# Each 512 KB weight chunk of a two-layer diffusion step loaded by two transfers of 256 KB

## What is computed

```python
for l in range(2):
    mc, ml = adaln(c_ctx, ada_w[l], ada_b[l]), adaln(c, ada_w[l], ada_b[l])   # shift, scale, gate, twice
    h = modulate(x, norm_mix[l], shift, scale)             # RMS norm, then scale and shift
    y = retention_mixer(h) if l == 0 else windowed_attention(h)
    x = x + gate * y
    h = modulate(x, norm_ffn[l], shift2, scale2)
    x = x + gate2 * conv_ffn(h)                            # 1024 -> 2 x 2816, conv of 3, silu(g) * u, -> 1024
y = rmsnorm(x, norm_final)
```

## Time and profile before

| | |
|---|---|
| median of 3 runs | 2172.25 us (2169.92 to 2173.08) |
| the profiled execution's own time | 2175.08 us |
| its span in the trace | 2173.3 us |
| TensorE matmul busy | 2057.9 us, 95% of the span |
| queue of the weight stream (q1) | 171.99 MB in 47232 packets, 23.1% of 16 engines' span |
| mean granted TensorE clock | 0.97 |

### The profile page before, as it was taken

One profiled execution on the slowest core, in us unless ns is written; L12 is line 12 of the kernel. 1 busy time (PEld: TensorE's weight loads), 2 busy tenths in 40 slices (PEclk: granted clock), 3 DMA queues, 4 the chain that ended last, 5 costly groups with the idle time before them and its releaser, 6 DMA issues.

```text
span 2173.3 us, 32383 instructions
## 1 busy us (share of the span) xinstructions
PE 2057.9 (95%) x12472; PEld 1809.2 (83%) x12472; DVE 925.8 (43%) x1299; ACT 654.1 (30%) x1280; POOL 758.0 (35%) x477
## 2 busy tenths in 40 slices
PE   5899999999999998999999999997779999999998
PEld 3776888598688757999999999984449999999998
DVE  1511410340242044762464364654441774575473
ACT  2522212223222224331232233334432432232232
POOL 1433233233323323333233334336654333333332
PEclk9899999999999998999999999898989999999999
DMA  6432232223123201432432342220002122222211
GB/s 238 171 136 78 97 107 78 77 91 105 68 98 116 68 29 40 154 137 78 145 115 102 113 144 69 75 74 1 1 1 68 52 79 78 73 77 78 68 68 49
DMA packets 52265, 190.02 MB, mean 87 GB/s; under 512 B 5825, under 2 KB 6977, under 8 KB 51521
## 3 DMA queue, kind: packets, MB, share of 16 engines
q1 hardware_dynamic: 47232, 171.99, 23.1%
q10 hardware_dynamic: 4928, 16.53, 2.0%
HBM read 181.41 MB, written 7.08 MB: 87 GB/s over the span
## 4 chain that ended last, share of the span: by engine, by line
PE 88%; DVE 3%; issue 3%; ACT 2%; DMA 1%; POOLq 1%; POOL 1%; DVEq 1%; ACTq 0%; SPq 0%
PE ps L350 35%; PE ps L389 21%; PE ps L365 15%; PE ps L405 2%; PE ps L332 2%; PE ps L541 2%; PE ps L550 1%; PE ps L423 1%; DVE stat L1394 1%; PE ps L536 1%; PE ps L337 1%; PE ps L413 1%; PE ps L710 1%; ACT pr L1007 1%; POOLq L1077 1%
## 5 line engine op out<-in xcount | busy, mean ns | idle before, releaser
L1051 POOL TENSOR_TENSOR w_l<-raw,w_h 128x1024 fp32r<-128x1024 f32 x232 | 563.4, 2430 | 1173.9 <-ACT w_h L746 1173.6
L350 PE MATMUL ps<-h_h,w_h 128*128 128x320 f32 x1696 | 528.3, 311 | 3.1 <-issue 1.6
L350 PE MATMUL ps<-h_h,w_l 128*128 128x320 f32 x1696 | 524.7, 309 | 0.0
L350 PE MATMUL ps<-h_l,w_h 128*128 128x320 f32 x1696 | 524.7, 309 | 0.0
L746 ACT CAST w_h<-raw 128x1024 fp32r<-128x1024 f32 x232 | 245.5, 1058 | 580.9 <-PE ps L389 315.6
L350 PEld LDWEIGHTS ps<-h_h,w_h 128*128 128x128 f32 x1696 | 319.0, 188 | 16.4 <-issue 14.7
L350 PEld LDWEIGHTS ps<-h_l,w_h 128*128 128x128 f32 x1696 | 319.1, 188 | 0.2 <-issue 0.2
L350 PEld LDWEIGHTS ps<-h_h,w_l 128*128 128x128 f32 x1696 | 319.1, 188 | 0.0
L1344 DVE SCALAR_TENSOR_TENSOR cc<-ca,vec,cc 128x641 f32<-128x641 f32 x88 | 231.1, 2627 | 15.2 <-issue 15.2
L1203 DVE SCALAR_TENSOR_TENSOR xT<-ps,mods,xT 128x128 f32<-128x128 f32 (+2 forms) x264 | 107.8, 436 | 302.7 <-PE ps L389 302.7
L389 PE MATMUL ps<-m_l,w_h 128*128 128x320 f32 x704 | 216.8, 308 | 0.0
(11 more groups left out here) (183 smaller groups left out, 2720.1 us busy)
## 6 DMA issues: line engine op xcount, KB each, us to landing
raw<-stream_dram SPq DMA_DIRECT2D x328, 512.0 KB, 3.6
S<-state_dram ACTq DMA_DIRECT2D x4, 1024.0 KB, 7.7
new_state_dram<-st_out ACTq DMA_DIRECT2D x8, 512.0 KB, 3.1
xT<-x_dram ACTq DMA_DIRECT2D x1, 2560.0 KB, 12.1
y_dram<-aq ACTq DMA_DIRECT2D x8, 320.0 KB, 2.4
dm<-diff_dram ACTq DMA_DIRECT2D x1, 512.0 KB, 4.7
rope_t<-rope_t_dram ACTq DMA_DIRECT2D x1, 512.0 KB, 8.7
rope_a<-rope_a_dram ACTq DMA_DIRECT2D x1, 512.0 KB, 3.7
```

The lines of the kernel that those rows point to most:

```text
L350: mm = nc.tensor.matmul(ps[:, banks + half, 0:HALF], w, x[:, k, lo_hi(half)], start=(k == 0 and n == 0), stop=(k == KT - 1 and n == 2))
L1051: nc.gpsimd.tensor_tensor(w_l[:, r, :], raw[:, s, :], w_h[:, r, :].bitcast(F32), ALU.subtract).then_inc(raw_used[s], 1)
```

## The change

Every chunk is loaded by two transfers, partitions 0 to 63 and partitions 64 to 127, issued one behind the other on the same queue after the same wait. Both add 16 to the same semaphore, so its two waiters ask for 32 for each chunk. Nothing else is changed.

```diff
@@ -300,7 +300,8 @@
                 s = c % RAW
                 if turns is not None:
                     sp.wait_ge(raw_used[s], turns)
-                sp.dma_start(raw[:, s, :], dr["stream"][c + RAW * i]).then_inc(raw_landed[s], 16)
+                for rows in (slice(0, P // 2), slice(P // 2, P)):
+                    sp.dma_start(raw[rows, s, :], dr["stream"][c + RAW * i, rows]).then_inc(raw_landed[s], 16)
@@ -398,7 +399,7 @@
                 for kc in range(4):
                     s, n = b.chunk(b.ada[k0 + kc], i)
-                    pe.wait_ge(raw_landed[s], 16 * n)
+                    pe.wait_ge(raw_landed[s], 32 * n)
@@ -740,7 +741,7 @@
                 s, landed = b.chunk(b.at[j], i)
                 r, n = b.split(j, i)
-                act.wait_ge(raw_landed[s], 16 * landed)
+                act.wait_ge(raw_landed[s], 32 * landed)
```

## The result

The changed kernel takes 2194.03 us (median of 4 runs, 2186.75 to 2197.21) against 2172.36 us of the kernel before: a ratio of 1.0095, 95% interval 1.0075 to 1.0116. It is slower by 21.7 us by the medians, 16.3 to 25.2 by the interval. The forecast was 2187 (2173.5 to 2200): the direction and the mechanism are right; the forecast loss, 15 us, is two thirds of what came.

The account below looks back on a forecast made before the run. TensorE, busy 95% of the span, was taken as the bound, so loads matter only where it waits for them. FFN 7.2 + 0.2, retention 0.7 and start 7.3 sum to 15.4 us: 2172.25 + 15.4 = 2187.6, say 2187 us (2173.5 to 2200).

Parts of the forecast that it names:

- d: Added delay until a whole chunk has landed, taken as 0.9 us between bounds of 0.1 and 1.43, at half rate per half.
- The distance in a burst: Time between landings of chunks issued in a row: 1.43 us before, forecast 1.43 + 0.9 = 2.3 us.
- The start: Loads up to the first projection: chunk 11 4.4 us late, chunk 19 2.4, cst 0.5; together 7.3 us.
- for cst I add 0.5 us (0 to 2): At the start, cst shares the DMA engines with the four first chunks; its delay was put at 0.5 us.
- where TensorE wants it at 33.3: At the start, chunk 11 would land at 37.7 us but is wanted at 33.3: 4.4 us lost.
- The shift for chunk 19: Chunks 16 to 19, issued from 48.6 us: the fourth lands at 60.0 in place of 57.6, delaying the first projection 2.4 us.
- The retention: Four ada blocks whose last chunk has 0.84, 0.76, 0.39 and 0.87 us to spare: 0.7 us lost in all.
- the FFN: Layer 0: eight already waiting ada blocks pay 8 x 0.9 = 7.2 us; two with 0.88 and 0.74 us in hand, 0.2.
- a microsecond there is covered: ACT's waits for main chunks, which TensorE needs four main chunks later; a tile takes 7.1 us, so small delays cost nothing.
- Full rate for each half: Rival: 64 partitions load as fast as 128, delay 0.15 us, 2 us lost, 2174 us, not slower; chance 0.24.
- Fully one after the other: Rival: halves wholly serial, delay 1.43 us, bursts 2.86 us apart, 31 us lost, 2203 us; chance 0.18 for delay above 1.2.
- the sign that was named for "wrong": Around a chunk loaded alone, GB/s still reaching 400 and more would mean the half rate is wrong and time near 2174.

## Why the prediction was right, and where it fell short

*d, right.* The forecast took 0.9 us between bounds of 0.1 and 1.43; it is 0.95 (4.60 against 3.64). Its reason, half the rate for half the partitions, read off stores that were not a clean comparison, is borne out in kind: with even and odd partitions, and with the middle 64, the slow packets are gone. But the makeup was not as told. I put the difference down to the rate alone; the rate gives 0.6 us, and 0.3 us is a part that I had left out: a transfer of 64 partitions holds SP for 0.47 us and starts its packets 0.3 us later. That the chosen value came out right is partly luck: the rate was taken too dear, and the longer issue at nothing.

*The distance in a burst, right.* The four chunks of the second ada block land at 23.2, 25.6, 27.8 and 30.1 us, 2.3 us apart, as forecast. Its last was forecast at 28.5.

*The start, 9.1 us for 7.3: two terms mis-sized.* The step "for cst I add 0.5 us (0 to 2)" measured 1.5 us: TensorE's first block starts at 16.48 for 14.95, and chunk 4 is issued that much later. The other is "where TensorE wants it at 33.3". That is the first matmul that uses chunk 11. Its weight load, which waits for the chunk, starts at 32.40 before, 0.9 us sooner. Chunk 11 now lands at 38.96, 1.3 us later than forecast. So the third block ends 6.6 us later (40.93 for 34.33): 4.4 us of the forecast, 1.3 and 0.9. The chain of the changed kernel, 14 to 42 us, goes this way:

```profile
16.48 1.95 PE ps L406 x6
...
23.28 6.78 DMA raw<-stream_dram
30.10 1.84 PE ps L406 x4
...
32.75 6.21 DMA raw<-stream_dram
39.01 1.95 PE ps L406 x4
```

The forecast also left out chunks 0 to 3, which before were there when TensorE wanted them. The fourth now lands at 20.56, and its weight load starts 2.4 us later than at the pace of before (PE, 16 to 24 us):

```profile
16.48 3.95 PE L406 MATMUL ps<-raw,csil 128*32 128x512 f32 x12 [16.48 <-DMA cst<-cst_dram]
20.60 1.44 PE L406 MATMUL ps<-raw,csil 128*32 128x512 f32 x4 [0.17 <-DMA raw<-stream_dram]
```

This stall isn't on the chain: chunk 4 is released by the block's first matmuls, and the loads behind it are issued without a wait.

The shift for chunk 19 was right: issued 6.55 us later and landed 8.9 later, 2.4 us more. The last conversion ends at 67.5 in place of 58.6, and the first projection starts at 69.7 for 61.0, where the forecast had about 7 us. TensorE's clock, which I let move along, did not. The slow stretch (granted clock 0.50, 1.2 of 2.4 GHz) ends 5.4 us later, at 72.6 for 67.2, so less of the projection runs in it: from there to the fifth ada block it is 15.6 us for 17.3. Then from 87 to 97 us the granted clock averages 0.66, 6.8 us of the ten at 1.2 GHz and the others at 2.4, where before such a stretch lasts 3.4 us: from the fifth block to the sixth it is 30.8 us for 28.7. The two nearly cancel.

*The retention, 3.1 us for 0.7, and the FFN, 8.3 + 1.0 for 7.4: the same step failed, "with 0.84, 0.76, 0.39 and 0.87 us to spare" and "two have 0.88 and 0.74 us in hand".* I took the time in hand from the landing to the first matmul of the chunk. It is the weight load, though, that waits for the semaphore, and it is issued one chunk ahead of its matmul. The last weight loads of the same block, before and then after:

```profile
1043.62 0.14 PEld L405 LDWEIGHTS ps<-raw,csil 128*32 128x32 f32 x4 [0.30 <-issue]
1044.05 0.13 PEld L405 LDWEIGHTS ps<-raw,csil 128*32 128x32 f32 x4 [0.29 <-issue]
```

```profile
1059.65 0.12 PEld L406 LDWEIGHTS ps<-raw,csil 128*32 128x32 f32 x2 [0.31 <-issue]
1060.16 0.14 PEld L406 LDWEIGHTS ps<-raw,csil 128*32 128x32 f32 x4 [0.39 <-DMA raw<-stream_dram]
```

Before, the last chunk's weight load starts at 1044.05 and the chunk has landed at 1043.60: 0.44 us in hand, not 0.88. With 0.44 us less everywhere, the retention's four come to 0.5 + 0.6 + 0.9 + 0.5 = 2.5 us (measured inside the blocks: 0.3, 0.8, 0.8 and 1.0; three of these chunks landed 4.7 to 4.9 us after their issue, not 4.5) and the FFN's two to 0.5 + 0.6 (measured 0.5 and 0.6). The eight blocks that waited already paid 0.8 to 1.1 us each, as forecast, but for one: the block at 904.38 us pays 1.9. Its last chunk is issued 1.4 us before the block, where it was 2.3, and that is a second step that failed: that "a microsecond there is covered" for main chunks. The block before it, the 14th, follows the norm, and there ACT has caught up with the stream and waits for the next main chunk. That chunk landed 4.76 us after the 14th block's start and now lands 5.70 us after it, and ACT converts it 0.94 us later:

```profile
872.15 1.05 ACT L746 CAST w_h<-raw 128x1024 fp32r<-128x1024 f32 x1 [2.18 <-DMA raw<-stream_dram]
```

```profile
885.24 1.05 ACT L747 CAST w_h<-raw 128x1024 fp32r<-128x1024 f32 x1 [3.12 <-DMA raw<-stream_dram]
```

For the next 13 us the instructions of ACT, VectorE and GpSimd that stand behind it are 0.93 us later too, by both timelines. At the end is the conversion of GpSimd that frees the slot of the late chunk: it ends 23.29 us after the 14th block's start, for 22.37. TensorE's tiles have not moved: the next ada block starts 24.86 us after the 14th in both traces. So this block pays d twice, 0.93 + 0.95 us. The timeline of GpSimd, where the last two conversions now touch:

```profile
884.36 2.42 POOL L1051 TENSOR_TENSOR w_l<-raw,w_h 128x1024 fp32r<-128x1024 f32 x1 [6.03 <-ACT w_h L746]
887.21 2.52 POOL L1051 TENSOR_TENSOR w_l<-raw,w_h 128x1024 fp32r<-128x1024 f32 x1 [0.44 <-ACT w_h L746]
```

```profile
897.44 5.37 POOL L1052 TENSOR_TENSOR w_l<-raw,w_h 128x1024 fp32r<-128x1024 f32 x2 [6.03 <-ACT w_h L747]
```

*The rivals.* Full rate for each half is what the even and odd partitions do: 2178 us, where the rival had 2174. "Fully one after the other" (d = 1.43) did not occur. That TensorE regains nothing held; that layer 1 and the attention pay nothing held to within 0.7 us, which is inside the scatter of that stretch.

*The signs that were named.* Packets 52480: yes. Later half at 4.4 to 4.5 us: 4.5 to 4.6. Ada blocks of 3.1 to 3.3 us: 3.20. Waits near 10 us: 11.2. First projection about 7 us later: 8.7. GB/s near 200 for 2.4 us: only in the later part, after a first stretch that reaches 492. That stretch meets the sign that was named for "wrong", 400 GB/s and more, and yet the time is not near 2174: the sign did not tell the two cases apart.

## What to carry to other kernels

Cut a load along the free dimension, or not at all. Two column halves cost nothing here and the first lands 0.8 us sooner; two row halves cost 1%, because the data of the later half move at a lower rate and each half takes longer to issue. And read the time that a load has in hand at the weight load or whatever instruction holds the wait, not at the matmul behind it: a consumer with 0.4 us in hand and one with 0.9 look alike until the load gets later. Where the engine that converts the weights has caught up with the stream, as behind the norm here, the next load had no cover, though the main chunks elsewhere had.

## What was not expected of the hardware

A transfer of 64 partitions takes 0.47 us to issue and starts its packets 1.26 us after the issue; one of 128 takes 0.33 and 0.97. This holds for contiguous halves and for even and odd partitions alike; the middle 64, in three transfers, took 0.54 us and 1.32. Two transfers of 128 partitions and 256 KB land together as soon as one of 512 KB (3.55 against 3.61 us in the ten ada chunks), though the second is issued 0.52 us later.
